# A fused two-layer decoder trunk on one core: the first weight slot in halves of 256 tokens, most parameters later in the queue

## What is computed

```python
def rmsnorm(x, g):
    return x * lax.rsqrt(jnp.mean(x * x, axis=-1, keepdims=True) + EPS) * g
...
h = rmsnorm(x, norm_even[i])
proj = h @ w_in_even[i]
(qa, ka, va, ga, qi, ki, wi, qb, kb, vb, gb, lr) = _split(proj, EVEN_SPLIT)
...
z = lr @ w_gla_lr[i] + b_gla_lr[i]
```

## Time and profile before

| | us |
|---|---|
| median of 3 runs | 547.63 |
| lowest, highest of the 3 | 547.46, 2952.62 |
| the profiled execution's own time | 548.83 |
| its span in the trace | 547.1 |
| mean granted TensorE clock in it | 0.981 of full |

### The profile page before, as it was taken

How to read it: one execution, slowest core, us unless ns; L and a number is a source line. 1 busy time by engine, 2 the same in 40 slices (tenths; PEclk the granted TensorE clock), 3 DMA queues, 4 the chain that set the end, 5 groups by cost and what they waited for, 6 DMA issues and landing times.

```text
span 547.1 us, 7463 instructions
## 1 busy us (share of the span) xinstructions
PE 529.9 (97%) x2815; PEld 422.1 (77%) x2817; DVE 368.0 (67%) x759; ACT 236.2 (43%) x364; POOL 263.9 (48%) x136
## 2 busy tenths in 40 slices
PE   5899999999999899999999999999999999999995
PEld 5676788777777788787888889778777678798884
DVE  2695499769867355555471154999989999828715
ACT  4542843233211144544271355466555654246413
POOL 3381455755633053033006316599999997350701
PEclk9799999999999999999999999999999999969998
DMA  6255155222222022000072403603332222202004
GB/s 228 43 168 187 57 178 189 78 79 77 78 78 78 0 78 78 1 2 1 15 293 79 133 21 91 178 8 89 95 98 88 84 74 84 77 1 77 1 0 154
DMA packets 44652, 46.75 MB, mean 85 GB/s; under 512 B 4425, under 2 KB 33116, under 8 KB 44616
## 3 DMA queue, kind: packets, MB, share of 16 engines
q1 hardware_dynamic: 44616, 46.28, 26.9%
HBM read 44.03 MB, written 2.12 MB: 84 GB/s over the span
## 4 chain that ended last, share of the span: by engine, by line
PE 81%; DVE 8%; ACT 3%; POOL 2%; DMA 2%; issue 2%; SPq 1%; POOLq 0%; ACTq 0%
PE bank L1411 30%; PE bank L1431 28%; PE bank L1692 3%; PE bank L1528 3%; PE bank L1602 3%; DVE r_va L981 2%; PE bank L1578 2%; DMA w_raw<-in_w_in_even_dram 2%; DVE top L979 2%; PE bank L1680 2%; PE bank L1591 2%; DVE r_ob L965 1%; PE bank L1698 1%; POOL w_lo L509 1%; PE bank L1709 1%
## 5 line engine op out<-in xcount | busy, mean ns | idle before, releaser
L509 POOL TENSOR_TENSOR w_lo<-w_raw,w_hi 128x2048 fp32r<-128x2048 f32 (+1 forms) x35 | 158.6, 4534 | 175.7 <-ACT w_hi L621 174.7
L1411 PE MATMUL bank<-hT_hi,w_hi 128*128 128x512 f32 (+1 forms) x296 | 120.8, 408 | 0.3 <-POOL w_lo L509 0.3
L1411 PE MATMUL bank<-hT_lo,w_hi 128*128 128x512 f32 (+1 forms) x296 | 118.6, 401 | 0.0
L1411 PE MATMUL bank<-hT_hi,w_lo 128*128 128x512 f32 (+1 forms) x296 | 117.3, 400 | 0.0
L1431 PE MATMUL bank<-w_hi,hT_hi 128*128 128x512 f32 x256 | 104.2, 407 | 0.0
L1431 PE MATMUL bank<-w_hi,hT_lo 128*128 128x512 f32 x256 | 100.1, 391 | 0.0
L1431 PE MATMUL bank<-w_lo,hT_hi 128*128 128x512 f32 x256 | 99.9, 390 | 0.0
L621 ACT ACTIVATE w_hi<-w_raw 128x2048 fp32r<-128x2048 f32 (+1 forms) x35 | 65.7, 1879 | 45.2 <-PE bank L1431 37.1
L1240 DVE SCALAR_TENSOR_TENSOR bank<-r_va,pvec,bank 128x512 f32<-128x512 f32 x108 | 76.0, 750 | 0.9
L1411 PEld LDWEIGHTS bank<-hT_hi,w_hi 128*128 128x128 f32 (+1 forms) x296 | 56.2, 190 | 16.2 <-issue 2.9
L560 POOL TENSOR_TENSOR r_g<-r_g 128x512 f32<-128x512 f32 x48 | 62.0, 1291 | 12.6 <-ACT r_g L795 7.0
(11 more groups left out here) (202 smaller groups left out, 717.0 us busy)
## 6 DMA issues: line engine op xcount, KB each, us to landing
w_raw<-in_w_in_even_dram SPq DMA_DIRECT2D x14, 1024.0 KB, 5.2
w_raw<-in_w_in_odd_dram SPq DMA_DIRECT2D x16, 512.0 KB, 4.7
w_raw<-in_w_out_even_dram SPq DMA_DIRECT2D x4, 1024.0 KB, 8.2
w_raw<-in_w_in_odd_dram SPq DMA_DIRECT2D x4, 1024.0 KB, 5.1
w_raw<-in_w_out_odd_dram SPq DMA_DIRECT2D x4, 1024.0 KB, 5.0
r_x<-in_x_dram SPq DMA_DIRECT2D x4, 512.0 KB, 4.7
r_x<-bias_rows SPq DMA_DIRECT2D x4, 512.0 KB, 6.2
r_x<-in_x_dram SPq DMA_DIRECT2D x1, 2048.0 KB, 7.8
```

The costliest lines, as they stand in the source:

```text
L509: nc.gpsimd.tensor_tensor(v(w_lo[j % 3]), v(w_raw[j % 2]), v(w_hi[j % 3]).bitcast(F32), ALU.subtract).then_inc(lo_ready, 1)
L1411: ins = nc.tensor.matmul(proj_bank(g)[0:m, :], w[:, k, P * i:P * i + m], h[:, k, :], start=(n == 0), stop=(n == 3 * KC - 1))
```

## The change

The first slot is now worked on in halves of 256 tokens, as the second layer's is. What moves:

- Queue: x rows 0 and 1, `even_rows` (the norm's weight alone, 8 rows of 128), slot 0 in two row halves (512 KB each: chunks 0 to 3, chunks 4 to 7), x rows 2 and 3, slot 1, the other parameters (eight loads), slot 2, `rel_rows`.
- 36 instead of 50 matmuls at the start; one transpose of `even_rows` and a DVE copy to `even_scale` take the place of the parameters' gate.
- ACT: squares of rows 0 and 1, the high part of slot 0's first half, the high halves of tokens 0 to 255, squares of row 3, the high halves of tokens 256 to 511, `split_hi(1)`.
- DVE: also makes the high part of slot 0's second half and the squares of row 2 (one instruction with two inputs from SBUF), between the scalings; then low halves; the parameters' copies behind all of that.
- POOL: slot 0's low part in three pieces (1024, 512, 512 columns) between the inverse roots.
- PE: transposes by row block, slot 0 as 96 matmuls of 256 tokens, the parameters' transposes behind them.

```diff
-WARM_START, WARM_LN = 50, 8
+WARM_START, WARM_LN = 36, 8
...
-            for t in range(TB):
+            for t in (0, 1):
                 sp.dma_start(x_t[:, t, :], x_rows[t]).then_inc(x_in[t], 16)
...
+            sp.dma_start(even_rows[:], norm_even.rearrange("a (c p) -> (a c) p", p=P)).then_inc(even_in, 16)
...
+            sp.dma_start(raw_0[:, 0:4, :], src_0[:, 0:4, :]).then_inc(first_raw, 16)
+            sp.dma_start(raw_0[:, 4:KC, :], src_0[:, 4:KC, :]).then_inc(raw_in[0], 16)
+            for t in (2, 3):
+                sp.dma_start(x_t[:, t, :], x_rows[t]).then_inc(x_in[t], 16)
...
-            load(0)
+            load(1)
+            sp.dma_start(param_rows[0:CW, :], conv_w[0]).then_inc(params_in, 16)
...
+            load(2)
             sp.dma_start(rel_rows[:], rel_bias.rearrange("b h -> h b"),
...
+            rsqrt_row(0)
+            rsqrt_row(1)
             pool.wait_ge(first_hi, 1)
-            first_half_lo(0).then_inc(first_lo, 1)
-            pool.wait_ge(hi_ready, 1)
-            first_half_lo(P).then_inc(lo_ready, 1)
+            part_lo(0, 1024).then_inc(first_lo, 1)
+            rsqrt_row(2)
+            pool.wait_ge(second_hi, 1)
+            part_lo(1024, 1536).then_inc(first_lo, 1)
+            rsqrt_row(3)
+            part_lo(1536, 2048).then_inc(lo_ready, 1)
...
+            row_square(0, junk[0])
+            row_square(1, junk[1])
             act.wait_ge(first_raw, 16)
+            nc.scalar.activation(w_hi[0][:, 0:1024], w_raw[0][:, 0:1024], ACT.Copy).then_inc(first_hi, 1)
+            act.wait_ge(even_ready, 1)
+            half_high(0, 0, even_bank, even_row)
+            act.wait_ge(squares, 1)
+            row_square(3, junk[0])
+            half_high(0, 1, even_bank, even_row)
             split_hi(1)
...
+            whole_variance(0, 1)
+            dve.wait_ge(even_T, 1)
+            nc.vector.tensor_copy(even_scale[:], bank[2][:, 0:KC]).then_inc(even_ready, 1)
+            whole_variance(1, 2)
+            scale_rows(0, 1)
+            scale_rows(1, 2)
+            dve.wait_ge(raw_in[0], 16)
+            nc.vector.tensor_copy(w_hi[0][:, 1024:2048], w_raw[0][:, 1024:2048]).then_inc(second_hi, 1)
+            dve.wait_ge(x_in[2], 16)
+            nc.vector.tensor_tensor_reduce(out=junk[2], in0=x_t[:, 2, :], in1=x_t[:, 2, :], scale=1.0 / D, scalar=EPS,
+                                           op0=ALU.mult, op1=ALU.add, accum_out=stat[:, 2:3]).then_inc(var_ready, 1)
+            dve.wait_ge(even_ready, 1)
+            half_low(0, 0, even_bank, even_row, range(4))
+            scale_rows(2, 3)
+            half_low(0, 0, even_bank, even_row, range(4, KC))
+            whole_variance(3, 3)
+            scale_rows(3, 4)
+            half_low(0, 1, even_bank, even_row)
+            dve.wait_ge(params_T, 1)
+            nc.vector.tensor_copy(pvec[:], bank[7][:, 0:KC * NROW].rearrange(
...
+            def first_products(half, ks, q, begins=False):
...
+                w, h = ((wh, hT_hi), (wh, hT_lo), (wl, hT_hi))[q]
+                for k in ks:
+                    pe.wait_ge(hT_ready if q == 1 else hT_hi_ready, KC * half + k + 1)
+                    for i in range(2):
+                        ins = nc.tensor.matmul(proj_bank(i)[:, HALF * half:HALF * half + HALF], w[:, k, P * i:P * i + P],
+                                               h[:, k, HALF * half:HALF * half + HALF], start=(begins and k == 0),
...
             pe.wait_ge(first_hi, 1)
-            group_a(0, 0, hT_round=0)
+            first_products(0, range(4), 0, begins=True)
+            pe.wait_ge(second_hi, 1)
+            first_products(0, range(4, KC), 0)
+            pe.wait_ge(first_lo, 1)
+            first_products(0, range(4), 2)
+            first_products(0, range(4), 1)
+            even_rows_in(2)
+            first_products(0, range(4, KC), 1)
+            pe.wait_ge(first_lo, 2)
+            first_products(0, range(4, 6), 2)
             slot_ready(0)
-            group_a(0, 1)
+            even_rows_in(3)
+            first_products(0, range(6, KC), 2)
+            first_products(1, range(KC), 0, begins=True)
+            first_products(1, range(KC), 1)
+            first_products(1, range(KC), 2)
+            params_transposed()
             slot_ready(1)
             group_a(1, 0)
```

More of the change, by code:

```diff
@@ L275, in hybrid_trunk @@
         first_hi = sem("first_hi")
+        second_hi = sem("second_hi")
         first_lo = sem("first_lo")
@@ L390, in odd_bank, with even_bank @@
             return bank[b][:, HALF * (c % 2):HALF * (c % 2) + HALF]
+        def even_bank(half, c):
+            b = (4, 5, 6, 7)[c // 2] if half == 0 else (2, 3, 4, 5)[c // 2]
+            return bank[b][:, HALF * (c % 2):HALF * (c % 2) + HALF]
         def mixed_bank(n):
@@ L604, in split_hi @@
             def split_hi(j):
[L606 to L613, removed]
+                act.wait_ge(raw_in[j % 2], raw_full[j])
                 if j >= 3:
@@ L761, in row_squares @@
                     squared(t)
-            def odd_high(half):
-                for c in range(KC):
-                    act.wait_ge(hT_in_bank, 2 * KC + KC * half + c - c % 2 + 2)
-                    nc.scalar.activation(hT_hi[:, c, HALF * half:HALF * half + HALF], odd_bank(half, c), ACT.Copy,
-                                         scale=pvec[:, c, ROW_NO:ROW_NO + 1]).then_inc(hT_hi_ready, 1)
+            odd_row = lambda c: pvec[:, c, ROW_NO:ROW_NO + 1]
             for s_ in range(S_OE, S_ODD):
@@ L917, in _, with half_low @@
-            dve.wait_ge(pvec_ready, 2)
-            hT_low(0, range(KC), lambda n: n, lambda c: pvec[:, c, ROW_NE:ROW_NE + 1])
+            def half_low(base, half, half_bank, scale, chunks=range(KC)):
+                for c in chunks:
+                    dve.wait_ge(hT_hi_ready, base + KC * half + c - c % 2 + 2)
+                    cols = slice(HALF * half, HALF * half + HALF)
+                    nc.vector.scalar_tensor_tensor(
+                        out=hT_lo[:, c, cols], in0=half_bank(half, c), scalar=scale(c),
+                        in1=hT_hi[:, c, cols].bitcast(F32), op0=ALU.mult, op1=ALU.subtract).then_inc(hT_ready, 1)
@@ new lines, in whole_variance @@
+            def whole_variance(t, count):
+                dve.wait_ge(squares, count)
+                nc.vector.tensor_scalar(stat[:, t:t + 1], stat[:, t:t + 1], 1.0 / D, EPS, ALU.mult,
+                                        ALU.add).then_inc(var_ready, 1)
+            even_row = lambda c: even_scale[:, c:c + 1]
+            whole_variance(0, 1)
+            dve.wait_ge(even_T, 1)
+            nc.vector.tensor_copy(even_scale[:], bank[2][:, 0:KC]).then_inc(even_ready, 1)
+            whole_variance(1, 2)
@@ L1351, in keep_clock, with even_rows_in @@
                     nc.tensor.matmul(dst[:, 0:P], ident_bf[:], ident_bf[:], start=True, stop=True)
-            def rows_normed(n, t):
-                pe.wait_ge(normed, 2 * t + (1 if n < 4 else 2))
-                if n == 7:
-                    pe.wait_ge(pvec_ready, 2)
+            def even_rows_in(t):
+                half = t // 2
+                if half:
+                    pe.wait_ge(even_ready, 1)
+                    pe.wait_ge(hT_ready, 4)
+                for c in range(KC):
+                    pe.wait_ge(normed, 2 * t + (1 if c < 4 else 2))
+                    ins = nc.tensor.transpose(even_bank(half, c)[:, P * (t % 2):P * (t % 2) + P], hx(t, c), ident[:])
+                    if t % 2:
+                        ins.then_inc(hT_in_bank, 1)
@@ L1397, in group_a @@
                 passes = ((wh, hT_hi), (wh, hT_lo), (wl, hT_hi))
[L1398 to L1402 removed]
+                order = [(k, q) for k in range(KC) for q in range(3)]
                 for n, (k, q) in enumerate(order):
[L1404 to L1407 removed]
                     if n in between:
@@ L1427, in unit_b @@
                     k = ks[i]
-                    if hT_round is not None:
-                        pe.wait_ge(hT_ready, KC * hT_round + (i if first else 4 + i) + 1)
+                    if hT_base is not None:
+                        pe.wait_ge(hT_ready, hT_base + (i if first else 4 + i) + 1)
                     for q, (h, w) in enumerate(((hT_hi, wh), (hT_hi, wl), (hT_lo, wh))):
```

154 lines of the change are left out of this document (72 added, 82 removed).

## The result

The changed kernel takes 550.66 us (median of 5 runs, 550.54 to 550.88), the kernel before 547.63 in the same job (five runs; one of 2952.62, the other four 547.41 to 549.00). The ratio is 1.0046, 95% interval 1.0032 to 1.0061: slower by about half a per cent, which by the 2% bound is no change. Forecast were 550.6 and "within 2%".

The account below looks back on a forecast made before the run. PE, busy 97% of the span, was taken as the bound, so only slot 2's start counts: 41.0 against 38.0 is 3.0 us later, and 547.6 + 3.0 = 550.6 us. Range 546.0 to 554.5, within 2% at 0.97.

Parts of the forecast that it names:

- A clear gain of the change: Before slot 0, PE no longer waits for the parameters: first product near 10 instead of 19.68, slot 0 4.7 us earlier.
- The step that decides is here: In slot 0, DVE operations from SBUF to SBUF stand still beside POOL's three pieces; the last scalings end at 20.5.
- Second scaling of row block 1 behind POOL's first piece, done at 11.4 and not at 8.9: In slot 0's first half, DVE's scaling is held by POOL's 2.37 us low piece and ends at 11.4.
- The three pieces: POOL's low pieces of slot 0: 2.37 us, half of that, and 1.2 us, the last excluding DVE's final two scalings.
- What is late next. Slot 1.: Slot 1's low part waits behind xor, 32 copies and parameters: slot 1 starts at 33.5, slot 2's low part ready at 40.0.
- The clock: PE idles 5.3 us before slot 1; half clock there loses 0.8 to 2.7 us; slot 2's start taken as 41.0.
- The sum on the profiled execution: Slot 2 starting 3.0 us later added to the old profiled execution's 548.8 us gives 551.8.
- rival D: DVE's top-k chain and late small matmuls could take up or add 1 us; widens each case, no chance given.
- Rival A: DVE hardly waits for POOL in slot 0: slot 2 starts at 37.6, 0.4 us earlier, 547.2 us; chance 0.2.
- Rival C: conv_w or rel_rows lands late behind slot 1's pieces; with rel_rows at 32, 553.8 us; chance 0.05.
- Rival B: PE's clock is low in slot 0 too: slot 2 starts at 44, 6 us later, 553.6 us; chance 0.17.
- The thin stretch as one engine's work: From 9 to 14 in the old trace, one DMA engine takes all 31 rows of conv_w, 5 us; costed at nothing.

Follow-up runs that it names:

- piece1_late: lo12_first with POOL's first low piece of slot 0 (1024 columns) moved behind the inverse root of row block 2: 545.22 us, ratio 0.9936 to the kernel before.
- lo12_first: Changed kernel with POOL making slot 1's and slot 2's low parts ahead of its wait for the xor: 544.37 us, ratio 0.9921 to the kernel before.
- filled_gap: Changed kernel with 90 unused small matmuls on PE between the parameters' transposes and slot 1: 549.07 us, ratio 1.0025 to the kernel before.
- after_conv_split: Changed kernel with conv_w's 31 rows loaded by two DMAs of 16 and 15 rows: 550.41 us, ratio 1.0052 to the kernel before.
- warm_50: Changed kernel with 50 instead of 36 small matmuls at the start: 551.99 us, ratio 1.0059 to the kernel before.
- conv_w_16_15: Kernel before, with only conv_w's 31 rows loaded by two DMAs of 16 and 15 rows: 543.67 us against 548.92, ratio 0.9907.

## Why the prediction was right, and where not

The forecast named slot 2's start as the number to find, put it at 41.0, and said 550.6; measured are 41.55 and 550.66. The mechanism is the one that was forecast. That the median agrees to 0.1 us is partly luck: slot 2's shift was 3.5 us and T's 3.4, where 3.0 were forecast, and what took the rest back between T and the medians isn't shown.

- *"A clear gain of the change"*, slot 0 from 32.0 to 27.3: 27.5. The parameters' transposes done at 28.2: 28.3.
- *"The step that decides is here"*, DVE standing still while POOL works: right as a mechanism, shown by piece1_late. *"Second scaling of row block 1 behind POOL's first piece, done at 11.4 and not at 8.9"* was wrong. The first weight half landed 0.9 us later than forecast (8.0 for 7.1), POOL started at 9.14 only, and the scaling was over at 8.89. The copy of the high half took its place: 2.57 us and not 0.8, done at 12.04 against 12.1. So the sum held in part because one instruction of DVE had to meet POOL's piece, whichever it was, and in part by luck: by the prediction's own rows POOL's piece, begun near 8.2, ends near 10.5 and a scaling held by it near 11.0, not 11.4, and the copy near 11.8. The sum stood 0.3 above its own rows, the weight landed 0.9 later, and the held scaling fell away: these nearly cancel. The pace of a free copy, put at 0.8 as the lower bound, is 0.69; the squares, put at 1.2, are 1.21.
- *The three pieces.* Scaling of row block 2 at 15.76 (16.0), last scaling 19.93 (20.5, held by POOL's third piece for 1.0 us), high halves 3.03 (3.0), low halves 3.23 (3.3), 32 copies 2.39 (2.3), low part of slot 1 from 31.90, slot 1 at 33.55 (33.5), slot 2's low part done at 39.8 (40.0).
- *"What is late next. Slot 1."* Right, and shown: with the low parts moved ahead of the xor (lo12_first) the gap is gone and the kernel is 4.2 us faster than before.
- *The clock.* Loss forecast at 0.8 to 2.7 us in slot 1; slot 1 ended at 41.55 in that range, 2.5 us behind its full-clock end, and filled_gap puts what counts on T at 1.8. The value taken (41.0) was 0.55 too small.
- *The sum on the profiled execution.* 551.8 forecast, 550.54 measured, while the median came out. The term missed is the late half-clock stretch, which rival D gave "a us" and no sign: it is 1.7 us, in whole steps, and was short in this profile and long in the profile of before.
- *Rival A* (DVE hardly waits) is refuted by the copy's 2.57 us. *Rival C* (a parameter load or rel_rows late) by after_conv_split and by the changed kernel's own timeline: the parameters' transposes start at 27.48, as slot 0's products end, and the 32 copies at 28.79, right behind the parameters' copies. *Rival B* (a slow PE in slot 0) was partly true: the first 16 transposes ran at half pace until about 11.3, but behind them PE waited for DVE's copy; warm_50, which undoes the slow pace, starts slot 1 no earlier (33.85 against 33.55), where the rival had 6 us.
- *The thin stretch as one engine's work* was read rightly and put among the edits "at nothing". Its cause was worth 3.2 us by T and 5.2 by the medians (ratio 0.9907). The prediction asked what its move would cost, not what its cause was worth.

## What to carry to other kernels

When a step is moved to the front, list each instruction that stood behind the step it replaces, on every engine: here the gain of 4.6 us was real, and POOL's wait for the xor, untouched by the change, gave it all back. Follow that wait by one more link before believing a fix: moving one low part only moved the gap to the next slot. And before rearranging a kernel around a late load, ask why the load is late; a stretch with a DMA share of 0.08, about one engine of sixteen, pointed to a load of 31 rows that two lines mend.

## What the runs showed of the hardware that I had not expected

- *A slow pace that the clock's row doesn't show.* In the changed kernel the windows from 7 to 11.8 us give a granted clock of 1.00, yet four transposes of 128 columns take 1.06 to 1.11 us there, against 0.60 to 0.63 at 15.5. In the kernel before, four take 1.12 us at 17.11, in a stretch with the clock at 0.50, so it is the pace of half clock. Why the row doesn't show it is open. With 50 small matmuls ahead (warm_50) they take 0.66 and 0.60. At the start of a program the pace of a known instruction tells more than the row.
- *A half-clock stretch without idle time.* Late in the program PE is busy in every us, with one-column matmuls between large ones, and the clock falls to half for 10.2 or 6.8 us. By the model above it is worth 1.7 us between two executions, as much as half of this change.
- *An issue that blocks the queue.* An issue of a w_raw load takes 0.37 us as a rule. The two that end slot 1's loads kept SP for 7.07 us (4.76 to 11.83) in the changed kernel, so the parameters' loads behind them were issued from 11.88 on only. Here the cover was wide enough; a queue's order costs its issuing engine too. The length of such an issue is not the load's own alone: the two for slot 0 take 5.63 us in the kernel before (from 5.69) and 1.75 in conv_w_16_15 (from 6.39), where only the load of conv_w ahead of them differs. What SP waits for in them isn't shown. The row:

```profile
4.76 7.07 SPq L441 DMA_DIRECT2D w_raw<-in_w_in_even_dram  x2
```
